# Two key blocks in place of three for stick-breaking attention, guards that can call a fallback program, and a weight ring of sixteen half blocks

## What is computed

```python
z = jnp.einsum('bhqd,bhkd->bhqk', qb, kb) * scale
mask = kpos[None, :] < qpos[:, None]                       # strictly causal
log_keep = jnp.where(mask, jax.nn.log_sigmoid(-z), 0.0)    # log(1 - beta)
suffix = lax.cumsum(log_keep, axis=3, reverse=True) - log_keep
weights = jnp.where(mask, jnp.exp(jax.nn.log_sigmoid(z) + suffix), 0.0)
out = jnp.einsum('bhqk,bhkd->bhqd', weights, vb)
```

## Time and profile before

| | us |
|---|---|
| median of 3 runs | 2695.6 |
| lowest and highest of them | 2658.72, 3011.68 |
| the profiled execution, its own time | 2660.62 |
| its span on the slowest core (core 7) | 2659.0 |
| spans of all cores | 2643.1 to 2659.0 |
| TensorE busy on core 7 | 2559.8 (96%) |
| VectorE, ScalarE, GpSimd busy | 1555.2, 1119.1, 685.5 |

### The profile page before, as it was taken

The page is one execution under the profiler, slowest core; times in us unless marked ns, Lnnn a source line. Parts: engine busy times, 40 slices in busy tenths (PEclk is TensorE's granted clock), DMA queues, the critical chain, the costliest instruction groups (busy, mean ns, idle before and its releaser), DMA issues.

```text
span 2659.0 us, 38510 instructions; the slowest of 8 cores (2643.1 to 2659.0 us)
## 1 busy us (share of the span) xinstructions
PE 2559.8 (96%) x12392; PEld 1125.4 (42%) x12392; DVE 1555.2 (58%) x2133; ACT 1119.1 (42%) x1685; POOL 685.5 (26%) x1081
## 2 busy tenths in 40 slices
PE   5899999999999999999999999999999999999996
PEld 1344444444444444444444444444444443444443
DVE  2771337468674775436476533667776588854435
ACT  3335223464334642264333444236442364345432
POOL 2531111222112353621245211212322122311111
PEclk9999999999999999999999999999999999999998
DMA  6677884746454996855472233423564236533534
GB/s 137 152 151 159 185 188 114 160 109 140 125 125 109 166 199 131 206 159 168 124 223 79 72 101 102 135 72 93 129 136 131 76 85 133 117 103 111 161 113 148
DMA packets 237627, 354.05 MB, mean 133 GB/s; under 512 B 121072, under 2 KB 126576, under 8 KB 237424
## 3 DMA queue, kind: packets, MB, share of 16 engines
q0 software_dynamic: 77952, 227.92, 36.8%
q1 hardware_dynamic: 158896, 122.54, 18.0%
q10 hardware_dynamic: 576, 1.05, 0.1%
HBM read 298.26 MB, written 79.69 MB: 142 GB/s over the span
## 4 chain that ended last, share of the span: by engine, by line
PE 87%; DMA 4%; issue 3%; DVE 3%; POOL 2%; ACT 1%; SPq 0%; DVEq 0%; POOLq 0%; ACTq 0%
PE ps L1384 65%; PE ps L1498 19%; DMA ring<-wblk 2%; PE ps L2177 1%; PE ps L2134 1%; DMA ring<-wcm 1%; DMA h<-xT 1%; DVE xn L1400 1%; POOL X L1397 1%; POOL TT L1397 1%; ACT ps L1393 1%; DMA AT<-A 1%; DVE h L1397 0%; PE ps L2052 0%; SPq L1681 0%
## 5 line engine op out<-in xcount | busy, mean ns | idle before, releaser
L1384 PE MATMUL ps<-xn,ring 128*128 128x512 bf16 x5872 | 1312.0, 381 | 29.5 <-ACT XB L1393 7.7
L1384 PEld LDWEIGHTS ps<-xn,ring 128*128 128x128 bf16 x5872 | 564.9, 98 | 716.2 <-issue 60.2
L1397 DVE TENSOR_TENSOR h<-ps,h 128x512 f32<-128x512 f32 x816 | 552.3, 687 | 526.2 <-PE ps L1498 348.0
L1393 ACT ACTIVATE ps<-ps 128x512 f32<-128x512 f32 x632 | 366.7, 583 | 677.8 <-PE ps L1384 353.0
L1322 POOL DMA_DIRECT2D ring<-wsc x364 | 196.5, 540 | 733.1 <-PE ps L1384 483.3
L1498 PE MATMUL ps<-hid,ring 128*128 128x512 bf16 x1408 | 331.5, 380 | 9.5 <-DMA ring<-wcm 4.8
L1393 ACT ACTIVATE hid<-ps 128x512 bf16<-128x512 f32 x512 | 304.3, 598 | 40.2 <-ACT ps L1393 1.8
L1393 ACT ACTIVATE xn<-h 128x2048 bf16<-128x2048 f32 (+1 forms) x92 | 152.9, 1682 | 364.8 <-DVE h L1397 344.2
L1384 PE MATMUL ps<-hid,ring 128*128 128x512 bf16 x1280 | 281.2, 379 | 0.0
L1322 POOL DMA_DIRECT2D ring<-wcm x214 | 114.5, 536 | 574.6 <-PE ps L1384 283.4
L1498 PE MATMUL ps<-TT,ring 128*128 128x512 bf16 x1056 | 255.8, 380 | 5.7 <-ACT ps L1393 3.5
(11 more groups left out here) (85 smaller groups left out, 1311.3 us busy)
## 6 DMA issues: line engine op xcount, KB each, us to landing
ring<-wsc POOLq DMA_DIRECT2D x364, 256.0 KB, 3.1
ring<-wblk POOLq DMA_DIRECT2D x188, 256.0 KB, 5.7
ring<-wcm POOLq DMA_DIRECT2D x66, 512.0 KB, 4.1
ring<-wcm POOLq DMA_DIRECT2D x88, 384.0 KB, 3.8
wsc<-ring SPq DMA_DIRECT2D x124, 256.0 KB, 4.3
h<-xT SPq DMA_DIRECT2D x64, 256.0 KB, 7.2
wcm<-TT SPq DMA_DIRECT2D x64, 256.0 KB, 5.1
oT<-stg SPq DMA_DIRECT2D x56, 256.0 KB, 4.2
```

The source lines that it names most:

```text
L1384: ins = pe.matmul(out, lhsT=l, rhs=r, start=(i == 0), stop=(i == n - 1), **({"skip_group_check": True} if skip else {}))
L1393: return self.S.op("act", lambda e: e.activation(out=out, in_=in_, func=func, **kw), rd=rd, wr=wr, dur=0.17 + n * 0.00083, aset=aset)
L1397: return self.S.op(eng, lambda e: e.tensor_tensor(out=out, in0=a, in1=b, op=op), rd=rd, wr=wr, dur=dur)
```

## The change

- Attention looks at two key blocks, gi - 1 and gi. Scores, sigmoid, scan, differences, transposes and `fv` cover at most 256 columns a head; `Kh`, `Vh` and what is saved of K and V between the halves shrink to one block.
- What is left out is guarded three times. The window's product (now for gi > 1) must be at most 2^-70. For every position behind the first 256 of a sequence the squared attention output must be at least 2^-76: one Square on ScalarE and one running minimum `om` on VectorE at the end of every four units. A bound on V's weight columns, computed once in `vbound`, must be at most 3.9. If one fails, the fallback runs.
- The ring has 16 slots.
- x of sequence 1 is loaded in pairs of channel blocks, half as many DMAs of twice the size.
- `up_strassen` is rewritten to leave one bank by a buffer `cT`; it isn't called.

```diff
-RING = 12
+RING = 16
@@ attention
-                c0 = max(0, 2 - gi) * 128
+                c0 = max(0, 1 - gi) * 128
-                blocks = [gi - 2 + jj for jj in range(3)]
+                blocks = [gi - 1, gi]
...
-                self.act(k2[:, :, c0:384], z2[:, :, c0:384], AF.Sigmoid, zt, [tk], 2 * (384 - c0), aset="sig", scale=-0.125)
+                self.act(k2[:, :, c0:256], z2[:, :, c0:256], AF.Sigmoid, zt, [tk], 2 * (256 - c0), aset="sig", scale=-0.125)
...
-                         rd=[tk, self.t_fm], wr=[tC], dur=1.75)
+                         rd=[tk, self.t_fm], wr=[tC], dur=1.25)
...
-                if gi > 2:
+                if gi > 1:
...
-                     dur=1.4, dma=("AT", ai), nbytes=300000, lat=1.2)
+                     dur=1.2, dma=("AT", ai), nbytes=220000, lat=1.2)
...
                 if qb == 3:
                     self.cp("dve", mx[:, t, 4 + a, :], self.bap(pb), [self.t_bank[pb]], [tm[t][4 + a]], 0.69)
+                    q0 = 256 if gi < 8 and t == 0 else 0
+                    k = a % 2
+                    sq = self.sq[s][k]
+                    self.act(sq[:, q0:512], mx[:, t, 4 + a, q0:512], AF.Square, [tm[t][4 + a]], [self.t_sq[k]], 512)
+                    self.tt("dve", self.om[:, q0:512], self.om[:, q0:512], sq[:, q0:512], ALU.min, [self.t_sq[k], self.t_om],
+                            [self.t_om], 0.43)
@@ layer1_in, mov
+                        if which == 1 and s == 0 and p == 0:
+                            self.vbound(slots)
@@
+    def vbound(self, slots):
+        S = self.S
+        TT = self.TT[:].rearrange("p a b n -> p (a b) n")
+        for k in range(8):
+            self.act(TT[:, k, :], self.rs(slots[k]), AF.Square, [self.rt(slots[k])], [self.t_TT[k // 4][k % 4 // 2]], 512)
+        bi = self.bank("n")
+        self.mms(self.bap(bi), [(self.ones[:], TT[:, k, :]) for k in range(8)],
+                 self.t_TT[0] + self.t_TT[1] + [self.t_ones], [self.t_bank[bi]], MM8)
+        f = self.fl2
+        S.op("dve", lambda e: e.tensor_reduce(out=f[:, 2:3], in_=self.bap(bi), axis=mybir.AxisListType.X, op=ALU.max),
+             rd=[self.t_bank[bi]], wr=[self.t_vs], dur=0.7)
...
@@ load_x
+        w = 1 if s == 0 else 2
         for t in tiles:
-            for c in range(8):
+            for c in range(0, 8, w):
...
@@ flag
+        S.op("dve", lambda e: e.tensor_reduce(out=f[:, 1:2], in_=self.om[:], axis=mybir.AxisListType.X, op=ALU.min),
+             rd=[self.t_om], wr=[t1], dur=0.7)
+        self.ts("dve", f[:, 4:5], f[:, 0:1], CTAIL, None, ALU.is_gt, None, [t2], [t2], 0.1)
+        self.ts("dve", f[:, 5:6], f[:, 1:2], OFLOOR, None, ALU.is_lt, None, [t1], [t1], 0.1)
+        self.ts("dve", f[:, 6:7], f[:, 2:3], VCEIL, None, ALU.is_gt, None, [self.t_vs], [self.t_vs], 0.1)
...
```

More of the change, by code:

```diff
@@ L25 @@
 MM8 = 1.735
+CTAIL = 2.0 ** -70
+OFLOOR = 2.0 ** -76
+VCEIL = 3.9
 RB = 20.0
@@ L522, in _prep_new @@
     bsb = np.ascontiguousarray(np.broadcast_to(inp["sgu_b"][0].reshape(1, 512), (128, 512))).astype(np.float32)
-    floor = np.zeros((128, 2, 384), np.float32)
+    floor = np.zeros((128, 2, 256), np.float32)
     q = np.arange(128)[:, None]
     k = np.arange(128)[None, :]
-    floor[:, :, 256:] = (k >= q).astype(np.float32)[:, None, :]
+    floor[:, :, 128:] = (k >= q).astype(np.float32)[:, None, :]
     cb = np.concatenate([np.ones((128, 128), np.float32), inp["pool_w"][0].transpose(1, 0, 2).reshape(128, 512),
-                         floor.reshape(128, 768)], axis=1).astype(np.float32)
+                         floor.reshape(128, 512)], axis=1).astype(np.float32)
     return dict(ncf=cf, bsb=bsb, ncb=cb)
@@ L1205, in alloc @@
         self.ms = [new("ms%d" % i, [128, 512], F32)[0] for i in range(2)]
-        self.flags = new("flags", [128, 208], F32)[0]
+        self.flags = new("flags", [128, 224], F32)[0]
         self.fl2 = new("fl2", [128, 8], F32)[0]
@@ L1211, in alloc @@
         self.pah = [new("pah%d" % s, [128, 4, 16], F32)[0] for s in range(2)]
-        self.AT = [new("AT%d" % i, [128, 6, 128], BF16)[0] for i in range(NAT)]
+        self.AT = [new("AT%d" % i, [128, 4, 128], BF16)[0] for i in range(NAT)]
+        self.om = new("om", [128, 512], BF16)[0]
+        self.t_om = T()
+        self.t_vs = T()
         self.st6 = new("st6", [128, 8, 8], F32)[0]
+        self.cT = [new("cT%d" % i, [128, 512], F32, at=mx[0][1] + 12288 + i * 2048)[0] for i in range(2)]
         at = mx[1][1]
@@ L1587, in relu2, with add @@
                 self.act(hd[:, t, j, :], o, AF.Square, [tb], [td[t][j]], 512)
-            def add(dst, a, b):
-                x, y = st[a], st[b]
-                o = self.tt("dve", self.bap(st[dst]), self.bap(x), self.bap(y), ALU.add,
-                            [self.t_bank[x], self.t_bank[y]], [self.t_bank[st[dst]]], 0.69)
+            def add(out, tout):
+                x, i = st["b"], st["i"]
+                self.tt("dve", out, self.bap(x), self.cT[i][:], ALU.add, [self.t_bank[x]] + tm[1][4 + 2 * i:6 + 2 * i], tout, 0.69)
             def p1():
@@ L1603, in p5 @@
                 prod("c", 2, lambda i: m[:, 0, i, :], tm[0][0:4], True)
+                i = st["i"]
+                self.act(self.cT[i][:], self.bap(st["c"]), AF.Copy, [self.t_bank[st["c"]]], tm[1][4 + 2 * i:6 + 2 * i], 490)
             def p6():
                 prod("b", 3, lambda i: m[:, 0, 4 + i, :], tm[0][4:8], False)
-                add("d", "b", "c")
+                add(self.bap(st["d"]), [self.t_bank[st["d"]]])
             def p2():
@@ L1619, in p7 @@
                 prod("b", 5, lambda i: X[:, 1, i, :], tX[1][0:4], False)
-                add("c", "b", "c")
-                bi = st["c"]
-                self.stt(hd[:, 1, j2, :], self.bap(bi), 0.0, self.bap(bi), ALU.max, ALU.mult, [self.t_bank[bi]], [td[1][j2]])
+                i = st["i"]
+                tc = tm[1][4 + 2 * i:6 + 2 * i]
+                add(self.cT[i][:], tc)
+                self.stt(hd[:, 1, j2, :], self.cT[i][:], 0.0, self.cT[i][:], ALU.max, ALU.mult, tc, [td[1][j2]], dur=0.72)
             def p4():
@@ L1677, in load_x @@
     def load_x(self, s, p, tiles=(0, 1), after=()):
+        w = 1 if s == 0 else 2
         for t in tiles:
-            for c in range(8):
-                src = self.xT[s, c * 128:(c + 1) * 128, p * 1024 + t * 512:p * 1024 + (t + 1) * 512]
-                self.S.op("sp", (lambda t, c, src: (lambda e: e.dma_start(out=self.h[s][:, t, c, :], in_=src)))(t, c, src),
-                          rd=list(after), wr=[self.t_h[s][t][c]], dur=0.45, dma=("h", s, t, c), nbytes=262144)
+            for c in range(0, 8, w):
+                src = self.xT[s, c * 128:(c + w) * 128, p * 1024 + t * 512:p * 1024 + (t + 1) * 512].rearrange(
+                    "(a p) n -> p a n", a=w)
+                self.S.op("sp", (lambda t, c, src: (lambda e: e.dma_start(out=self.h[s][:, t, c:c + w, :], in_=src)))(t, c, src),
+                          rd=list(after), wr=self.t_h[s][t][c:c + w], dur=0.45, dma=("h", s, t, c), nbytes=262144 * w)
     def norm_tile(self, s, t, gcol, final=None, fine=False):
@@ L2077, in layer1_in @@
         return steps, last
+    def vbound(self, slots):
[9 more added lines that the diff above has]
+             rd=[self.t_bank[bi]], wr=[self.t_vs], dur=0.7)
+        g = self.cf[:, 16:24]
+        g2 = self.st6[:, 0, :]
+        self.tt("dve", g2, g, g, ALU.mult, [self.t_cf], [self.t_st6[0]], 0.1)
+        S.op("dve", lambda e: e.tensor_reduce(out=f[:, 3:4], in_=g2, axis=mybir.AxisListType.X, op=ALU.max),
+             rd=[self.t_st6[0]], wr=[self.t_vs], dur=0.1)
+        self.tt("dve", f[:, 2:3], f[:, 2:3], f[:, 3:4], ALU.mult, [self.t_vs], [self.t_vs], 0.1)
     def attention(self, s, p):
@@ L2175, in fv @@
                             vc = slice(a * 128 + hh * 64, a * 128 + hh * 64 + 64)
[L2176 removed]
+                            lt = self.V[:, b - p * 8, vc] if b >= p * 8 else self.Vh[:, vc]
                             ins = pe.matmul(self.bap(pb)[hh * 64:hh * 64 + 64, qb * 128:(qb + 1) * 128], lhsT=lt,
[L2178 removed]
+                                            rhs=self.AT[ai][:, hh * 2 + jj, :], start=(n == 0), stop=(n == len(vb) - 1),
                                             skip_group_check=True)
```

71 lines of the change are left out of this document (37 added, 34 removed).

## The result

The changed kernel takes **2632.3 us** (median of 4 runs, 2629.2 to 2633.4), beside a median of 2679.5 us for the kernel before on the same chip. The ratio of the undisturbed runs is **0.989** (95% interval 0.9866 to 0.9914): 29 us faster, where -17 us was forecast.

The account below looks back on a forecast made before the run. TensorE was taken to bound the kernel, busy 2559.8 of 2659.0 us. Terms -12.3 + 1.8 - 6 - 4 + 3.5 = -17 us took 2660.6 to 2643 us, 8 in 10 range 2614 to 2684.

Parts of the forecast that it names:

- The shorter stream: Attention on TensorE: 112 units each 0.11 us shorter from smaller `fz` and `fv`, -12.3 us.
- VectorE's shorter scans: Attention on VectorE: 57 us less scan work against 13 us more from the output guard, counted as 0.
- Waits for AT: Second attention stretch: smaller transposes, shorter scans and less queued DMA remove most waits and slow clock, -6 us (0 to -8.4).
- The ring: Strassen groups' loads: 16 slots give a third more lead, cutting ring waits and slow clock, -4 us (0 to -6.8).
- The V bound: Ahead of attention: `vbound` puts 8 matmuls of 512 columns into TensorE's stream once, +1.8 us.
- The output guard: 32 Squares on ScalarE and 32 minima on VectorE, outweighed by the shorter scans, 0 us.
- The start: Kernel start: two cast loads go beside x, so x and TensorE come later, +3.5 us (0 to 8).
- The new order: Whole kernel: replanned engine orders put small waits elsewhere with about the same sum, 0, 8 us either way.
- The pairs: Paired x loads of sequence 1: same bytes, fewer issues, counted at nothing; a late pair would cost about 5 us.
- Waits fall widely: Rival: VectorE and ScalarE relieved in all four attention stretches, ring deeper everywhere, 2614 us; chance 0.14.
- It saves nothing in the end: Rival: stream 10.5 us shorter, but waits remain and start and new order cost 8 us each, 2666 us; chance 0.14.
- The guard fires: Rival: an output at or near zero sends a core through the fallback, over 5100 us in all; chance 0.04.

Follow-up runs that it names:

- e5: e3 with scans as long as before, 768 elements, 256 of them without use; fastest run 2642.4 us, spans -10.3 us against the kernel before, no ratio.
- e3: The changed kernel with only the shorter attention window: ring of 12, single x loads, no output guard, no V bound; ratio 0.9919 to the kernel before.
- e4: The kernel before with all its work, its planner told the changed attention durations; fastest run 2648.4 us, spans -3.1 us, no ratio.
- e1: The changed kernel with the ring put back from 16 to 12 slots; ratio 0.9937 to the kernel before.
- e9: The changed kernel with a ring of 14 slots in place of 16; ratio 0.9906 to the kernel before.
- e2: The changed kernel without the output guard and the bound on V's weights; ratio 0.9896 to the kernel before.
- e8: The changed kernel with the two additional early cast loads held until a later norm input; fastest run 2633.1 us, spans -23.1 us against the kernel before, no ratio.
- e10: The changed kernel, only its planner told that sequence 1's first x loads take 1.3 times as long; ratio 0.9921 to the kernel before.
- e6: e3 with transposes as wide as before, 768 elements a row, the last 256 zeros; ratio 0.9928 to the kernel before.

## Why the prediction was right, and which of its terms were not

The time (2643 forecast, 2632 measured) and the direction came out; the gain was forecast at 17 us and is 29, because the ring's term was far too small, VectorE's relief was put at nothing, and no term was far too large.

- **The shorter stream, -12.3: right in its parts.** The distances after are those of the smaller units before (0.22 and 0.23 us), 0.11 us less a unit, by subtraction of 0.22 + 0.23 from 0.27 + 0.29. And the attention stretches without waits and clock (the last column of e5's table) are shorter by 12.7 us in e3. What the stretches gain is more, for the next reason. The Trainium skill (TensorE: Matmul & The Clock Gate, section "Wait — 56ns, not 53.3ns?") gives 55.6 ns for one 128-column matmul; by it, the four of `fv` one behind the other would take 0.222 us and six 0.33 us, both estimates. The trace agrees for four (0.23 us from start to start after) and not for six (0.29 in the earlier trace rows): two matmuls more cost 0.05 or 0.06 us. So the agreement at four is no proof of the rule: a part that doesn't depend on the count, and about 0.03 us for each matmul, fit both. That the two heads' matmuls overlap is one reading of it, which no run tests.
- **"So 0" for VectorE's shorter scans: wrong, in a sum that held by its other terms.** The 57 us less on VectorE were set only against the guards' 13 us. They are worth about 4 us of TensorE's time in one order (e4 against e3), and up to 9 with another order's share in it (e5 against e3). The waits of TensorE for `DVE h`, 4.2 us in 8 pieces, stood in the list of before below those of the earlier trace rows; I gave them no row and no price, and the earlier trace rows, which the prediction names for them, doesn't show them. Each kernel has one profile, so every such part is good to some 2 us.
- **Waits for AT, -6: gone, with the right sum but partly the wrong cause.** No wait for AT is left after, and the window behind the second stretch has a clock of 1.00 in place of the 0.63 of the earlier trace rows:

```profile
1012.00:1019.50 7.50, 7.50 (x36) 3.42 (x35) 3.44 (x6) 0.63 (x1) 1.09 (x2) 1.00 0.25 50
```

  But e3, with all the smaller transposes and scans, still waits 3.4 us for AT, e1 0.8 and e9 5.8. So the size of a transpose alone doesn't decide whether one is late; that the order and the ring's loads do is likely, but wasn't tried apart. As a mean of the 8 cores of before, AT waits were 3.3 us in the attention stretches, and of 2.8 us of clock lost there 0.9 are left, which makes 5.2 us; core 7, from which I took 8.4, had more than the mean.
- **The ring, -4 (bounds 0 and -6.8): mis-sized.** It measures 13.9 us in spans, 16 in marks and 12.5 by the ratios, with the order that was planned for it. I had priced it by the waits that name it (4.8 us) and the clock of one window. The window of the earlier trace rows is indeed better after:

```profile
1185.00:1251.50 66.50, 66.13 (x302) 29.84 (x307) 44.95 (x69) 28.49 (x45) 12.78 (x24) 1.00 0.56 176
```

  TensorE is idle for 0.4 us there, where it was for 3.2, and the clock is 1.00, not 0.97. That is 4.8 us, in line with 4.3 at the marks. What was missed is that the ring also gains near 2500 us, 2.8 at the marks, and that attention gains by it too, 6.1 us.
- **The V bound, +1.8: right** (1.6 measured). **The output guard, 0: right as far as is known** (e2). What it would cost with the old scans wasn't tried.
- **The start, +3.5: a near size by a wrong mechanism.** Two more loads do go beside x, but x isn't later (33.2 against 33.7 us), and e8 gains nothing. In their place 2.1 us are lost between marks 56 and 360, by a planned order in which ScalarE waits for x with bank copies behind it. e10 shows it by moving the order alone. That belongs to "elsewhere with about the same sum". That +3.5 came near 2.1 is luck.
- **The new order, 0, 8 either way: right in size.** e4 gives -3 to -5 us, most of it in one piece at 2000 to 2042 us.
- **The pairs, 0: not measured apart.** (The 5 us for a late pair name, where a load takes 6.0; nothing hangs on it.)
- **The whole.** -17 stands against -29. The ring alone brings some 9 us more than its term and the scans some 4, which is about the difference. The number fell into the range by its width, not because the waits were read rightly.
- **The rivals.** "Waits fall widely" (2614 us) is the nearest in kind to what happened: 2632 lies between it and the forecast (2643). Its argument against itself held: the third stretch, full already in the earlier trace rows, gave the least, 4.7 us. "It saves nothing in the end" and "The guard fires" didn't come.

Three things stay open. Stretch 2 takes 172.1 us on all eight cores after, while before it took 175.9 to 185.5, e3 172.0 to 177.1, e5 173.4 to 182.7 and e6 172.2 to 181.2; that stalls in it fall on each core differently is shown, why is not. How the 6.1 us of the ring in attention split is known in part: between e1 and after, TensorE's waits there fall by 5.0 us (mean of the cores), of which only 1.6 name ring loads or transposes, and 1.8 name VectorE's `vnb` at the head of the stretches; those are gone with 14 slots as well, and whether by the ring or by the order isn't known. And pairs of x alone weren't measured.

## What to carry to other kernels

Price an engine at 57% by who is queued behind its longest instruction, not by its share: 0.5 us off each of some 120 scans was worth about 4 us on another engine. An experiment that adds even a memset may move a planner's whole order, so compare the orders before you read the time. Price a deeper buffer in every stage that uses it, not by the waits that name it in one list; the time at which the same k-th weight load begins, compared over cores and kernels, shows at once which stage pays. And where a planner orders an in-order queue, an input that lands later than it assumes stands in front of everything queued behind it: a slightly longer assumed duration for that load moved 4.5 us at the start.

## What had not been expected of the hardware

The end of the kernel is longer by some 2 us: from the cast of the flag to the last instruction 10.2 us before (core 7) and 12.1 after (core 2). The piece that differs is GpSimd's last drain. On all cores it takes 4.66 to 4.71 us in the seven kernels with 12 slots, 6.21 to 6.25 in the six with 16 and 6.54 to 6.58 in the one with 14 (e9). So it depends on the ring but isn't in proportion to its size, and e9, from which about 5.5 us was expected, contradicts the simple reading (more semaphores, more time). It takes back 1.5 of the 16 us that the ring gives; its cause is open.
